# Router on un-normalised rows, the first expert's rows taken by a one-hot matmul, and the bias split and table steps moved in a fused conv, attention and mixture-of-experts block

## What is computed

```python
h = h + mixed @ w_out                       # 512 x 1024
hn = rms_norm(h, norm_ffn_g)
logits = hn @ router_w + router_b           # 32 experts
top_vals, top_idx = top_k(logits, 4); gates = softmax(top_vals)
# each token's row goes to its 4 experts; per expert:
gu = x @ w_gate_up[e] + b_gate_up[e]        # 1024 -> 2048
act = min(gu[:, 0::2], 7) * sigmoid(1.702 * ...) * (clip(gu[:, 1::2], -7, 7) + 1)
y = act @ w_down[e] + b_down[e]             # 1024 -> 1024, times the gate, added to h
```

## Time and profile before

| | us |
|---|---|
| median of three runs (1485.42 to 1486.91) | 1485.84 |
| the profiled execution's own time | 1486.37 |
| its span, first to last instruction | 1484.7 |
| last product of the attention output, to first product of the first expert | 281.98 to 318.91 |
| first expert's eight up-chunks, bias and bias_down | 318.91 to 359.23 |
| first product of the loop's first body | 362.61 |
| one expert in the loop | 35.24 |

### The profile page before, as it was taken

The page is one execution under the profiler, slowest core; times in us unless marked ns, Lnnn a source line. Parts: engine busy times, 40 slices in busy tenths (PEclk is TensorE's granted clock), DMA queues, the critical chain, the costliest instruction groups (busy, mean ns, idle before and its releaser), DMA issues.

```text
span 1484.7 us, 20096 instructions
## 1 busy us (share of the span) xinstructions
PE 1418.3 (96%) x6498; PEld 1143.8 (77%) x6498; DVE 1235.6 (83%) x1074; ACT 1006.7 (68%) x1014; POOL 264.8 (18%) x280
## 2 busy tenths in 40 slices
PE   6998969879999999999999999999999999999995
PEld 4887447766888888888888888888888888888884
DVE  4688665566999999999989999999999999989994
ACT  5248265443777777777777777777777777777773
POOL 3000000054011112211211111122221122221111
PEclk9999979867999999999999999999999999999998
DMA  7412003658999999999999999999999999999971
GB/s 242 151 55 85 1 1 126 240 132 284 353 380 364 380 381 368 369 377 372 373 364 373 371 364 371 384 358 369 386 358 382 370 357 369 377 374 369 367 292 21
DMA packets 96842, 445.74 MB, mean 300 GB/s; under 512 B 14895, under 2 KB 19007, under 8 KB 63920
## 3 DMA queue, kind: packets, MB, share of 16 engines
q1 hardware_dynamic: 82752, 421.82, 75.2%
...
HBM read 439.96 MB, written 22.43 MB: 311 GB/s over the span
## 4 chain that ended last, share of the span: by engine, by line
PE 93%; DVE 3%; ACT 1%; DMA 1%; issue 1%; SPq 0%; POOL 0%; ACTq 0%; POOLq 0%; DVEq 0%
PE psum L1318 27%; PE psum L1319 27%; PE psum L1320 27%; PE psum L1609 2%; PE psum L1403 2%; PE psum L1618 2%; PE psum L1635 1%; DMA ring<-in_w_in 1%; PE psum L1644 1%; PE psum L1538 1%; PE psum L1476 1%; PE psum L1417 0%; DVE wlo L1215 0%; PE psum L1436 0%; PE psum L1556 0%
## 5 line engine op out<-in xcount | busy, mean ns | idle before, releaser
L1215 DVE TENSOR_TENSOR wlo<-ring,whi 128x2048 fp32r<-128x2048 f32 x384 | 871.6, 2290 | 109.7 <-ACT whi L783 105.9
L783 ACT ACTIVATE whi<-ring 128x2048 fp32r<-128x2048 f32 x384 | 737.2, 1920 | 195.0 <-PE psum L1320 195.0
L1318 PE MATMUL psum<-whi,xT_hi 128*128 128x512 f32 x1024 | 403.6, 394 | 6.2 <-DVE wlo L1215 3.4
L1319 PE MATMUL psum<-whi,xT_lo 128*128 128x512 f32 x1024 | 400.5, 391 | 0.0
L1320 PE MATMUL psum<-wlo,xT_hi 128*128 128x512 f32 x1024 | 400.3, 391 | 0.0
L1318 PEld LDWEIGHTS psum<-whi,xT_hi 128*128 128x128 f32 x1024 | 193.6, 189 | 46.7 <-DVE wlo L1215 3.8
L1320 PEld LDWEIGHTS psum<-wlo,xT_hi 128*128 128x128 f32 x1024 | 193.5, 189 | 40.5
L1319 PEld LDWEIGHTS psum<-whi,xT_lo 128*128 128x128 f32 x1024 | 193.6, 189 | 39.1
L1318 PE MATMUL psum<-whi,aT_hi 128*128 128x512 f32 x512 | 202.0, 395 | 1.9 <-ACT y_sb L809 1.9
L1320 PE MATMUL psum<-wlo,aT_hi 128*128 128x512 f32 x512 | 199.6, 390 | 0.0
L1319 PE MATMUL psum<-whi,aT_lo 128*128 128x512 f32 x512 | 199.5, 390 | 0.0
...
## 6 DMA issues: line engine op xcount, KB each, us to landing
ring<-in_w_gate_up SPq DMA_DIRECT2D x256, 1024.0 KB, 7.6
ring<-in_w_down SPq DMA_DIRECT2D x128, 1024.0 KB, 7.0
ring<-in_w_in SPq DMA_DIRECT2D x10, 1024.0 KB, 11.3
ring<-in_w_out SPq DMA_DIRECT2D x4, 1024.0 KB, 4.9
h<-in_x SPq DMA_DIRECT2D x4, 512.0 KB, 5.7
hn_rows<-hn ACTq DMA_DIRECT2D x4, 512.0 KB, 3.2
out<-h ACTq DMA_DIRECT2D x4, 512.0 KB, 8.2
...
```

The lines of the kernel that those rows point to most:

```text
L783: nc.scalar.activation(whi[:, hi_of(number), :], ring[:, slot(number), :], ACT.Copy).then_inc(hi_ready, 1)
L1215: TT(wlo[:, slot(number), :], ring[:, slot(number), :], whi[:, hi_of(number), :].bitcast(F32), ALU.subtract).then_inc(lo_ready, 1)
L1318: MM(o, s_hi, m_hi, start=first, stop=False)
L1319: MM(o, s_lo, m_hi, start=False, stop=False)
```

## The change

The router's matrix is scaled once by norm_ffn_g, and its products take h1 rather than hn, with the matrix as the stationary operand (32 columns) and the turned rows moving (128); 1/rms is applied to the logits. The result is 32 x 128, so ACT copies it out (logits_out) and PE turns it back (turn_lg). Ranks take fp32r operands. The first expert's rows are no longer gathered: DVE makes a one-hot of 128 places for each tile (position), and PE multiplies hn with it in float32 into the two banks from which xT is split (first_rows). Token lists for the experts 1 and 2 (next_lists, first_slots_of), the counts and item tables, the places, gates and the turned gates stand between the first expert's chunks. `b_raw` and `b_split` live in ring slots 4 and 5, are loaded and split before and between add_rest calls, and POOL moves the result to `b_hl` by a DMA.

```diff
-        b_raw = at("b_raw", [P, 2 * FF], F32, r0 + 36864)
+        b_raw = at("b_raw", [P, 2 * FF], F32, 4 * CW * 4)
...
+        b_split = at("b_split", [P, 2 * FF], F32R, 5 * CW * 4)
...
+                if m == PER_ITEM - 2:
+                    sp.wait_ge(bhl_ready, 2)
                 if m == PER_ITEM - 1:
-                    sp.wait_ge(xg_loaded, 16)
+                    sp.wait_ge(bhl_moved, 16)
...
+                small(gffn_k, norm_ffn_g.rearrange("(k p) -> p k", p=P))
...
+            pool.wait_ge(logits_done, T)
+            pool.wait_ge(bhl_ready, 2)
+            pool.dma_start(b_hl[:, :], b_split[:, :]).then_inc(bhl_moved, 16)
+            pool.wait_ge(sel0_ready, T * (AHEAD - 1))
             nc.gpsimd.memset(xg[:, :], 0.0).then_inc(xg_cleared, 1)
             pool.wait_ge(slot0_ready, 1)
-            gather(0, slot0_i[:, 0:1])
-            scatter_rows(0)
-            scatter_rows(1)
             gather(1, slot0_i[:, 1:2])
-            scatter_rows(2)
-            scatter_rows(3)
+            for t in range(T):
+                scatter_rows(t)
             gather(2, slot0_i[:, 2:3])
...
+            for part in range(4):
+                act.dma_start(b_raw[part * E:(part + 1) * E, :], b_gate_up).then_inc(braw_loaded, 16)
...
+            act.wait_ge(bhl_one, 1)
+            nc.scalar.activation(b_split[:, :], b_raw[:, :], ACT.Copy).then_inc(bhl_hi, 1)
...
+            def logits_out(t):
+                act.wait_ge(lgT_done, t + 1)
+                if t >= 1:
+                    act.wait_ge(logits_done, t)
+                nc.scalar.activation(lgT[:, :], bank(LOGITS[t])[0:E, 0:P], ACT.Copy).then_inc(lgT_evac, 1)
...
             root(0)
             root(1)
             turned(0)
             store(0)
             root(2)
+            logits_out(0)
...
             turned(2)
+            logits_out(1)
             turned(3)
             store(2)
+            logits_out(2)
             store(3)
+            logits_out(3)
             act.wait_ge(chunk_used, N_FRONT)
+            act.dma_start(b_dn[:, :], b_down).then_inc(b_dn_loaded, 16)
             gates_exp(1)
+            hi_item(0, 0)
+            hi_item(0, 1)
             gates_exp(2)
-            for part in range(4):
-                act.dma_start(b_raw[part * E:(part + 1) * E, :], b_gate_up).then_inc(braw_loaded, 16)
-            act.dma_start(b_dn[:, :], b_down).then_inc(braw_loaded, 16)
+            hi_item(0, 2)
...
-            for k in range(FIRST_HI):
+            xgT_out(0)
+            hi_item(0, FIRST_HI)
+            hi_item(0, FIRST_HI + 1)
+            for k in range(FIRST_HI + 2, UP):
                 hi_item(0, k)
             act.wait_ge(gdT_done, 1)
-            nc.scalar.activation(gateT[:, :, :], bank(7)[0:E, :].rearrange("p (t c) -> p t c", t=T),
+            act.wait_ge(hn_stored, 16 * T)
+            nc.scalar.activation(gateT[:, :, :], bank(4)[0:E, :].rearrange("p (t c) -> p t c", t=T),
                                  ACT.Copy).then_inc(gdT_evac, 1)
-            xgT_out(0)
-            act.wait_ge(braw_loaded, 80)
-            act.wait_ge(bhl_one, 1)
-            act.wait_ge(hn_stored, 16 * T)
-            nc.scalar.activation(b_hl[:, :], b_raw[:, :], ACT.Copy).then_inc(bhl_hi, 1)
-            for k in range(FIRST_HI, UP):
-                hi_item(0, k)
             hi_item(0, UP + 0)
             hi_item(0, UP + 1)
             sigmoid(0)
...
+            TT(rw[:, :, :], rw[:, :, :], gffn_k.unsqueeze(2).to_broadcast([P, KT, E]), ALU.mult).then_inc(rw_scaled, 1)
...
-                link(TT(lg[:, t, :], bank(LOGITS[t])[:, 0:E], rb[:, :], ALU.add))
+                link(STT(out=lg[:, t, :], in0=bank(LOGITS[t])[:, P:P + E], scalar=rstd2[:, t:t + 1], in1=rb[:, :],
+                         op0=ALU.mult, op1=ALU.add))
...
+                COPY(mask_r[:, t, :], mask[:, t, 0, :]).then_inc(mask_ready, 1)
+                COPY(mask[:, t, 1:3, :], mask[:, t, 0:1, :].to_broadcast([P, 2, E])).then_inc(mask_copied, 1)
+            def position(t):
                 dve.wait_ge(rank_done, t + 1)
                 if t == 0:
                     dve.wait_ge(e96_ready, 2)
-                link(STT(out=rank0[:, t, 0:AHEAD], in0=bank(RANKS[t])[:, 0:AHEAD], scalar=1.0, in1=mask[:, t, 0, 0:AHEAD],
-                         op0=ALU.add, op1=ALU.mult))
-                for e in range(AHEAD):
-                    TS(sel0[:, t, e, :], slot_no[:, :], rank0[:, t, e:e + 1], None, ALU.is_equal).then_inc(sel0_ready, 1)
+                link(TT(pos[:, t, :], bank(RANKS[t])[:, 0:E], row_e[:, :], ALU.add))
+                TS(sel_rows[:, t, :], place_no[:, 0, :], pos[:, t, 0:1], mask[:, t, 0, 0:1], ALU.is_equal,
+                   ALU.mult).then_inc(rows_chosen, 1)
+            def next_lists():
+                for t in range(T):
+                    for e in range(1, AHEAD):
+                        TS(sel0[:, t, e - 1, :], place_no[:, e, :], pos[:, t, e:e + 1], mask[:, t, 0, e:e + 1], ALU.is_equal,
+                           ALU.mult).then_inc(sel0_ready, 1)
...
+            one_more()
+            add_rest(0)
+            normalise(0)
+            bias_low(slice(E, 2 * E))
+            add_rest(1)
+            normalise(1)
+            bias_low(slice(3 * E, P))
+            add_rest(2)
+            normalise(2)
+            choose(0)
+            add_rest(3)
+            normalise(3)
+            position(0)
+            choose(1)
+            choose(2)
+            position(1)
+            choose(3)
+            position(2)
+            position(3)
+            lo_item(0, 0)
+            split_xgT(0)
+            lo_item(0, 1)
+            next_lists()
+            lo_item(0, 2)
+            dve.wait_ge(slot0_done, 1)
+            TS(slot0_i[:, 1:AHEAD], bank(4)[:, 497:496 + AHEAD], float(NOWHERE), None, ALU.add).then_inc(slot0_ready, 1)
...
+            lo_item(0, 3)
+            flags()
+            lo_item(0, 4)
+            place(0)
             places()
-            lo_item(0, 0)
+            lo_item(0, 5)
+            place(1)
             items()
-            lo_item(0, 1)
-            split_xgT(0)
-            one_more()
-            for k in range(2, UP):
-                lo_item(0, k)
-                if k == FIRST_HI:
-                    dve.wait_ge(bhl_hi, 1)
-                    for low in (slice(E, 2 * E), slice(3 * E, P)):
-                        TT(b_hl[low, :], b_raw[low, :], b_hl[low, :].bitcast(F32), ALU.subtract).then_inc(bhl_ready, 1)
-                    dve.wait_ge(items_ready, 1)
-                    pick(0, sel_up, sel_up_ready, None)
-            dve.wait_ge(bhl_ready, 2)
+            lo_item(0, 6)
+            place(2)
+            place(3)
+            dense_gates(0)
+            dense_gates(1)
+            pick(0, sel_up, sel_up_ready, None)
+            lo_item(0, 7)
+            dense_gates(2)
+            dense_gates(3)
             lo_item(0, UP + 0)
             clip(0)
...
-            def turn_hn(t):
-                pe.wait_ge(hn_ready, t + 1)
+            def turn_h1(t):
+                pe.wait_ge(h1_done, t + 1)
                 if t >= 1:
                     pe.wait_ge(hnT_evac, t)
                 for k in range(KT):
-                    ins = nc.tensor.transpose(bank(0, 2)[:, k * P:(k + 1) * P], hn[:, t, k * P:(k + 1) * P], ident[:, :])
+                    ins = nc.tensor.transpose(bank(0, 2)[:, k * P:(k + 1) * P], h1[:, t, k * P:(k + 1) * P], ident[:, :])
                 ins.then_inc(hnT_done, 1)
...
-                    ins = MM(bank(LOGITS[t])[:, 0:E], hnT[:, t % 2, k * P:(k + 1) * P], rw[:, k, :],
+                    ins = MM(bank(LOGITS[t])[0:E, 0:P], rw[:, k, :], hnT[:, t % 2, k * P:(k + 1) * P],
                              start=(k == 0), stop=(k == KT - 1))
-                ins.then_inc(logits_done, 1)
+                ins.then_inc(lgT_done, 1)
+            def turn_lg(t):
+                pe.wait_ge(lgT_evac, t + 1)
+                nc.tensor.transpose(bank(LOGITS[t])[:, P:P + E], lgT[:, :], ident[0:E, 0:E]).then_inc(logits_done, 1)
...
+            def first_rows(t):
+                pe.wait_ge(rows_chosen, t + 1)
+                pe.wait_ge(hn_ready, t + 1)
+                if t == 0:
+                    pe.wait_ge(h1_done, T)
+                for half in range(2):
+                    for k in range(4):
+                        d = (half * 4 + k) * P
+                        ins = MM(bank(6 + half)[:, k * P:(k + 1) * P], hn[:, t, d:d + P], sel_rows[:, t, :],
+                                 start=(t == 0 and k == 0), stop=(t == T - 1 and k == 3))
+                    if t == T - 1:
+                        ins.then_inc(xgT_done, 1)
             out_rows(0)
             out_rows(1)
-            turn_hn(0)
+            turn_h1(0)
             out_rows(2)
             logits(0)
-            turn_hn(1)
+            turn_h1(1)
+            turn_lg(0)
             out_rows(3)
             ranks(0)
+            turn_h1(2)
             logits(1)
-            turn_hn(2)
-            turn_hn(3)
```

(40 more changed lines are left out.)

191 lines of the change are left out of this document (91 added, 100 removed).

## The result

| | before | after |
|---|---|---|
| median of 20 runs, us | 1485.72 (1484.37 to 1487.37) | 1487.81 (1484.11 to 1493.39) |
| ratio to before, 95% interval | 1 | 1.0016, 1.001 to 1.0022 |
| the profiled execution's own time | 1486.37 | 1487.32 |
| its span | 1484.7 | 1485.7 |

The change makes the kernel 2.1 us slower, where 3 us of gain were forecast. The time lies in the range of 1478.0 to 1488.5, on the wrong side of no change. What follows compares the traces stage by stage, from one event to the next and not by absolute times: even ahead of the first changed step the profiled run of after is 1.07 us earlier (o_tok at 248.30, before at 249.37).

What follows compares the result with a forecast made beforehand. PE, always busy at full clock, bounds the expert loop, so only its start moves: 2.0 + 1.6 - 17.1 + 1.5 + 8.3 = -3.7 on 1486.37 gives 1482.7 us, range 1478.0 to 1488.5.

Steps and rivals of the forecast that it cites:

- the late bias rows: Ahead of out_rows(3): the bias rows' load lands after 260.8 and delays the chain, +1.6 us, from 0.7 to 3.5.
- the stretch behind the last wlo: From the last up-chunk's wlo to the loop's first body: 24.1 us against 15.8, +8.3, with two bias_down tiles at half clock.
- What bounds it: In the expert loop PE is always busy at full clock; the change only moves when the loop's first body starts, 362.61.
- the three stretches: Before the loop: out_rows(3), 276.27 to 281.98; 36.9 us to the first expert's first product; 43.7 us to the first body.
- Ahead of out_rows(3), the chain (+2.0): PE's turn_lg(0) now waits for logits_out(0) behind the third tile's root, so out_rows(3) starts at 278.2, not 276.27: +2.0 us.
- The rival with late rows: Bias rows land at 264.6, the wait before out_rows(3) grows to 5 us, 1.7 more at half clock; 1486.0, chance 0.20.
- To the first expert (-17.1): Out_rows(3) to the first expert's first product: 19.8 us against 36.9, without lists, places, tables, gather and half clock: -17.1.
- nothing is gained by the swap itself: Router products with 32 columns held and 128 moving take 1.75 us, at or a little below the 1.86 and 2.01 forms.
- The rival at half clock from the router on: PE at half clock from the router to the first rows: +8.5 us on the sum, 1491.2, slower; chance 0.14.
- The first expert's chunks (+1.5): From the first expert's first product to the last wlo, DVE is late: 29.4 us against 27.9, +1.5.
- The 19.7 for this stretch at full clock: Alternative behind the last wlo: with bias_down(2) and (3) at full clock, 19.7 us instead of 24.1, +3.9.

Runs made afterwards that it cites:

- a1_early: The changed kernel, with the bias rows' four loads issued early by SP instead of by ACT behind g_ffn; 1480.65 us, ratio 0.9965.
- c1_unswap: Changed kernel with bias rows loaded early and gateT copied behind whi and sigmoid, but router products as before (turned rows held, 32 columns moving); 1480.71 us.
- e1_unswap7: a7_all, but with the router's products as before: turned rows held, 32 columns moving, no copy or turning back; 1474.26 us, ratio 0.9922.
- a7_all: Changed kernel with bias rows loaded early, gateT behind whi and sigmoid, place(2) and (3) behind the last wlo, bias_low halves moved; 1472.03 us, ratio 0.991.
- d2_fill: a7_all, but bias_down's products contract over 128 rows instead of 32, the added rows being zeros; 1465.85 us, ratio 0.986.

## Why the prediction was wrong

Two terms of the sum failed: the late bias rows, put at 1.6 and worth 5.4, and the stretch behind the last wlo, put at 8.3 and worth 11.7. Either alone takes the gain of 3.7 to about nothing.

**What bounds it** was right: the loop took no part, and the three stretches carried everything.

**Ahead of out_rows(3), the chain (+2.0): right.** a1_early has this chain without late rows. Out_rows(3) starts at 277.12, 0.85 after that of before, in a run whose o_tok is 1.23 earlier (248.14): 2.1.

**The late bias rows (+1.6): this step failed.** Measured it is 7.45 - 2.1 = 5.4. I had two prices, an even share of the bandwidth (landing at 261.5) and the share that g_ffn's row gives (264 to 265), and took a value between them. They landed at 265.06, as the row said; 4.7 us of it is the wait (add_rest(0) at 265.67, in a1_early at 260.81 with an o_tok 0.16 earlier). The other 0.7 is ACT's copy of the rows, which stands ahead of root(0): behind the same end of add_rest(0) the square starts 0.7 later than in a1_early. The rival with late rows had added 1.7 for products at half clock. The half clock came (logits(0) took 3.60 us), but off the path, since turn_lg(0) waits for ACT. By the Trainium skill's page DMA: Bandwidth & Descriptors (Queues, rings and completion order) each engine takes turns between queues, a packet at a time, which I had read as an even share of the bytes; no run here shows the turns, and the rows landed 3.6 us later than that share gives, so the ring's chunks got more, and why is open. A row for a neighbour on the same queue, beside the same traffic, should not have been averaged with a rule. That rival was on paper, with a chance of 0.20 and its landing at 264.6.

**To the first expert (-17.1): right** at -17.7, with the times of its parts (router product 1.84, first rows 2.03). But its sentence that nothing is gained by the swap itself was wrong: the form costs the same at one clock, but with the old form the stretch is at half clock for a part. The rival at half clock from the router on did not occur; with the old form some 4 of its 8.5 us come back (3.6 in c1_unswap, 4.2 in e1_unswap7).

**The first expert's chunks (+1.5): measured 0.** The waits came ahead of the chunks named, at 0.4, 1.0 and 3.2 us in place of 0.6, 1.9 and 4.0.

**Behind the last wlo (+8.3): measured +11.7; this step failed too.** The steps are the ones named, in their order: gateT, two whi, table, sigmoid, add, bias_down(2). What was missed is chunk 7, put at full clock (2.8): it took 5.4, and bias_up and turning 0.3 more, since the clock had fallen behind the 3.2 us wait ahead of it, a wait that I had myself put at 4.0. The half clock in bias_down(2) and (3) was right (7.2, forecast 6.8), but not for the reason given. I had laid it to 4 us of idle time, of which 2.4 came; a7_all falls to half clock there with no wait over 0.9 us from chunk 7 on, and d2_fill with the same waits does not, so the 32 rows bring it without idle time. The 19.7 for this stretch at full clock is 1.0 under 24.1 less the 3.4 named there; the prediction did not list what makes that up, and transposes at full clock (1.09 us in d2_fill, not 1.97) would cover 0.9 of it.

**The sum.** -3.7, and 3.8 for the rows, 3.4 for the tail, -1.5 for the chunks, -0.6 for the way to the first expert, 0.1 each for the chain and out_rows(3), and -1.07 that this run was ahead beforehand, give +0.5: the body's start. The half clock in the body adds the rest to the span's +1.0. The medians differ by 2.1, since the profiled run of before lay 0.65 above its own median and that of after 0.5 below.
